# Five stage transitions worked in two groups of 256 tokens, with two weight remainders per transition on GpSimd

## What is computed

```python
# first block (FF = 2816; a 3x3 depthwise convolution over the 8 x 64 grid of tokens)
x  = x + g1 * (merge(...) @ w_out)                         # output stage
h2 = rmsnorm(x) * gain * (1 + scale) + shift               # transition A
x  = x + g2 * ((silu(z1) * z2) @ ffn_down)                 # z1, z2 = conv(h2 @ ffn_up)
x  = rmsnorm(x) * final_g                                  # sums of the "final norm"
# second block: retention with context keys, SwiGLU, short convolution, SwiGLU
ax = rms_norm(x, norm_mix) * (1 + sc) + sh                 # transition B
x  = x + g1 * ((silu(g) * o) @ w_o)                        # four heads
fx = modulate(rms_norm(x))                                 # transition C
x  = x + g2 * swiglu(fx, w1, w3, w2)
ax = modulate(rms_norm(x))                                 # transition D
x  = x + g1 * ((b_gate * conv3(c_gate * xv)) @ w_conv_out) # b, c, xv = ax @ w_conv_in
fx = modulate(rms_norm(x))                                 # transition E
x  = x + g2 * swiglu(fx, w1, w3, w2); out = rms_norm(x) * final_norm
```

## Time and profile before

| | us |
|---|---|
| median of 3 runs | 2410.75 |
| the profiled execution | 2411.24 |
| its span, first to last instruction | 2409.5 |

### The profile page before, as it was taken

The page is one execution under the profiler, slowest core; times in us unless marked ns, Lnnn a source line. Parts: engine busy times, 40 slices in busy tenths (PEclk is TensorE's granted clock), DMA queues, the critical chain, the costliest instruction groups (busy, mean ns, idle before and its releaser), DMA issues.

```text
span 2409.5 us, 29333 instructions
## 1 busy us (share of the span) xinstructions
PE 2305.6 (96%) x10276; PEld 1862.6 (77%) x10276; DVE 1395.6 (58%) x2056; ACT 874.8 (36%) x1168; POOL 162.6 (7%) x96
## 2 busy tenths in 40 slices
PE   7999999989999989999999998999998998999998
PEld 3788888768887868787778776888886886888886
DVE  4556856669999766654745547555435445333322
ACT  4533433245554333323323234443223233443322
POOL 0000000026664000000000000000000000000000
PEclk9999999999999999999999998999999999999999
DMA  6442214413334624142332323666532332333322
GB/s 270 131 136 74 71 57 151 152 57 105 89 102 140 192 80 146 55 129 88 104 116 74 106 79 124 192 190 199 157 93 65 105 96 63 105 94 104 96 88 70
DMA packets 72944, 273.82 MB, mean 114 GB/s; under 512 B 8096, under 2 KB 8480, under 8 KB 71456
## 3 DMA queue, kind: packets, MB, share of 16 engines
q1 hardware_dynamic: 53424, 199.74, 26.7%
q10 hardware_dynamic: 19440, 72.96, 9.6%
HBM read 270.57 MB, written 2.10 MB: 113 GB/s over the span
## 4 chain that ended last, share of the span: by engine, by line
PE 90%; DVE 5%; issue 2%; ACT 2%; DMA 1%; ACTq 0%; DVEq 0%; POOL 0%; SPq 0%
PE bank L424 85%; PE bank L765 1%; PE bank L862 1%; DVE rstd L472 1%; DVE rv_lo L1979 0%; DVE hx_lo L480 0%; PE bank L455 0%; DMA ident<-in_ident 0%; DVE tnorm L487 0%; PE bank L659 0%; PE bank L457 0%; DVE rstd L1799 0%; DVE std L449 0%; DVE rt L1930 0%; PE bank L944 0%
## 5 line engine op out<-in xcount | busy, mean ns | idle before, releaser
L424 PE MATMUL bank<-hx_hi,w_hi 128*128 128x512 f32 x1792 | 711.6, 397 | 40.2 <-DVE hx_lo L480 35.0
L424 PE MATMUL bank<-hx_hi,w_lo 128*128 128x512 f32 x1792 | 704.0, 393 | 0.0
L424 PE MATMUL bank<-hx_lo,w_hi 128*128 128x512 f32 x1792 | 703.9, 393 | 0.0
L383 DVE TENSOR_TENSOR w_lo<-w_raw,w_hi 128x1024 fp32r<-128x1024 f32 x306 | 374.8, 1225 | 495.2 <-ACT w_hi L375 488.9
L375 ACT ACTIVATE w_hi<-w_raw 128x1024 fp32r<-128x1024 f32 x350 | 369.0, 1055 | 458.1 <-PE bank L424 416.3
L424 PEld LDWEIGHTS bank<-hx_hi,w_hi 128*128 128x128 f32 x1792 | 340.7, 190 | 116.6 <-issue 41.1
L424 PEld LDWEIGHTS bank<-hx_hi,w_lo 128*128 128x128 f32 x1792 | 339.9, 190 | 72.4
L424 PEld LDWEIGHTS bank<-hx_lo,w_hi 128*128 128x128 f32 x1792 | 340.6, 190 | 71.0 <-issue 1.2
L1859 DVE SCALAR_TENSOR_TENSOR bank<-zpad,cols,bank 128x512 f32<-128x512 f32 x352 | 233.8, 751 | 11.7 <-ACT bank L1388 11.7
L424 PE MATMUL bank<-hid_hi,w_hi 128*128 128x512 f32 x528 | 210.1, 398 | 1.5 <-POOL hid_lo L2156 1.5
L424 PE MATMUL bank<-hid_lo,w_hi 128*128 128x512 f32 x528 | 209.8, 397 | 0.0
(11 more groups left out here) (305 smaller groups left out, 2752.3 us busy)
## 6 DMA issues: line engine op xcount, KB each, us to landing
w_raw<-in_wstream SPq DMA_DIRECT2D x350, 512.0 KB, 3.6
ada_raw<-in_ada_nk ACTq DMA_DIRECT2D x128, 512.0 KB, 3.7
ada_w<-in_ada_kn SPq DMA_DIRECT2D x8, 1024.0 KB, 18.8
dec<-in_dec ACTq DMA_DIRECT2D x4, 960.0 KB, 4.6
x_tok<-in_x SPq DMA_DIRECT2D x1, 2048.0 KB, 7.8
out_x<-out_tok SPq DMA_DIRECT2D x4, 512.0 KB, 4.0
crow<-in_crow SPq DMA_DIRECT2D x3, 512.0 KB, 23.1
ctx_tok<-in_ctx SPq DMA_DIRECT2D x1, 1024.0 KB, 9.9
```

Of the source, the lines that this page charges most:

```text
L383: nc.vector.tensor_tensor(w_lo[nb.at % RING][:], w_raw[nb.at % RAW][:], w_hi[nb.at % RING][:].bitcast(F32), ALU.subtract).then_inc(lo_read ...
L424: ins = nc.tensor.matmul(out_ap, s, m, start=first and at == 0, stop=last and at == n - 1)
```

## The change

The last output tile (B, D) or the last two (A, C, E) of the stage before a transition are worked in two halves of 256 tokens: first the first halves of all of them, then the second halves, which go to another bank (`bw`). The first half's update, squares, sums, root, reciprocal, scaling, `hx_hi` and `hx_lo` are done by themselves, in instructions 256 wide, and the sums of the first half stand in PE's queue after four k of the second halves. The next stage begins with three weight tiles in turn instead of two: for the first 256 tokens k = 0 and 1 of two tiles, then of the third, then k = 2 to 7 of all three, then all k for the second 256 tokens; the sums of the second half stand behind k = 2, and in B those of the final norm too. ACT and DVE have the second half's work between that of the first (`transition_act`, `transition_dve`). The root's table is loaded before the last squares. `w_lo` of the third and fourth blocks of the next stage (in C of the fourth alone) is written by GpSimd (`split_block`). The third tile of A goes to `by[0]`, that of B to `bw[0]`, and B's context keys come after all four tiles. The first round of the loops on ACT and DVE is written out where blocks are split elsewhere, the short convolution's loop is unrolled, and the final norm's scratch lies at other addresses. The transition at the start of the kernel and the one at its end stay.

```diff
+            def __init__(self, sems, scratch, past=(), last=0):
 
                 (self.sq_ready, self.summed, self.mm, self.root, self.rec, self.scaled, self.hi, self.lo) = sems
-                self.once, self.tiles, self.split_tiles, self.sums = n, KT * n, KT * split, (KT - 2) * n
                 self.sq, self.std, self.rooted, self.rstd = scratch
-
+                self.last = last
+                self.once = sum(2 if m else 1 for m in past)
+                self.tiles, self.halved = KT * self.once, sum(past)
+                self.squares, self.sums = sum(KT + m for m in past), sum(KT - 2 + (m == 2) for m in past)
...
+        last_halved = (0, 2, 1, 2, 1, 2, 0)
+        n1x, n2, nmx, nffn0, nmix1, nffn1, nf2 = (
+            Norm(shared, (sq, std, std, rstd), last_halved[:n], last_halved[n]) for n in range(7))
...
+        def half_sums_pe(pe, nm, h):
+
+            cut = HALF[h]
+            pe.wait_ge(nm.summed, nm.sums + KT - 2 + (h if nm.last == 2 else 0))
+            nc.tensor.matmul(bn[:, cut], ones[:], nm.std[:, cut], start=True, stop=False)
+            pe.wait_ge(nm.sq_ready, nm.squares + KT + nm.last * h)
+            nc.tensor.matmul(bn[:, cut], ones[:], nm.sq[(KT - 1) % 2][:, cut], start=False, stop=True).then_inc(nm.mm, 1)
+
+        def last_tiles_pe(pe, nm, tiles, both=0, sums_at=3):
+
+            def step(at, n, h):
+                dst, second, terms = tiles[at]
+                b, t, hi, lo = terms[n]
+                if h == 0 and (n == 0 or t == 0):
+                    pe.wait_ge(lo_ready, b.count(1))
+                wh, wl = wtile(b, t)
+                return three((dst, second)[h][:, HALF[h]], [(wh, wl, hi[:, HALF[h]], lo[:, HALF[h]])],
+                             n == 0, n == len(terms) - 1)
+
+            for n in range(both):
+                for h in range(2):
+                    ins = step(0, n, h)
+                if tiles[0][2][n][1] == KT - 1:
+                    ins.then_inc(block_done, 1)
+            for at in range(len(tiles)):
+                for n in range(both, len(tiles[at][2])):
+                    ins = step(at, n, 0)
+                ins.then_inc(half_done, 1)
+            for at in range(len(tiles)):
+                for n in range(both, len(tiles[at][2])):
+                    ins = step(at, n, 1)
+                    if tiles[at][2][n][1] == KT - 1:
+                        ins.then_inc(block_done, 1)
+                    elif n == len(tiles[at][2]) - 1:
+                        ins.then_inc(wo_half, 1)
+                    if at == 0 and n == both + sums_at:
+                        half_sums_pe(pe, nm, 0)
+
+        def first_tiles_pe(pe, nm, jobs, beside=lambda k: None):
+
+            def step(job, k, h):
+                b, dst, ends = job
+                wh, wl = wtile(b, k)
+                ins = three(dst[:, HALF[h]], [(wh, wl, hx_hi[:, k, HALF[h]], hx_lo[:, k, HALF[h]])], k == 0, k == KT - 1)
+                if ends and h == 1 and k == KT - 1:
+                    ins.then_inc(block_done, 1)
+
+            for b, _, _ in jobs[:2]:
+                pe.wait_ge(lo_ready, b.count(1))
+            for k in range(2):
+                pe.wait_ge(nm.lo, nm.tiles + k + 1)
+                for job in jobs[:2]:
+                    step(job, k, 0)
+            pe.wait_ge(lo_ready, jobs[2][0].count(1))
+            for k in range(2):
+                step(jobs[2], k, 0)
+            for h in range(2):
+                for k in range(2 if h == 0 else 0, KT):
+                    pe.wait_ge(nm.lo, nm.tiles + KT * h + k + 1)
+                    for job in jobs:
+                        step(job, k, h)
+                    if h == 0 and k == 2:
+                        half_sums_pe(pe, nm, 1)
+                        beside(k)
+
+        def transition_act(act, nm, job, shift, first_block, eps=eps_col, scale=None, extra=None):
+
+            def last_square(j, h):
+                nc.scalar.activation(nm.sq[j % 2][:, HALF[h]], res[:, j, HALF[h]], ACT.Square,
+                                     scale=1.0 if scale is None else scale[:, j:j + 1]).then_inc(nm.sq_ready, 1)
+
+            def root(h):
+                act.wait_ge(nm.mm, nm.once + h + 1)
+                nc.scalar.activation(nm.std[:, HALF[h]], bn[:, HALF[h]], ACT.Sqrt, scale=1.0 / D, bias=eps[:])\
+                    .then_inc(nm.root, 1)
+
+            def hi(j, h):
+                act.wait_ge(nm.scaled, nm.tiles + KT * h + j + 1)
+                nc.scalar.activation(hx_hi[:, j, HALF[h]], tnorm[j % 2][:, HALF[h]], ACT.Identity, bias=shift(j))\
+                    .then_inc(nm.hi, 1)
+
+            last = range(KT - nm.last, KT)
+            nc.scalar.activation(table_col[:], eps_col[:], ACT.Sqrt)
+            act.wait_ge(nm.summed, nm.sums + KT - 3)
+            for n, j in enumerate(last):
+                act.wait_ge(half_added, nm.halved + n + 1)
+                last_square(j, 0)
+            root(0)
+            if nm is not nffn0:
+                split_hi(act, Block(first_block - 1))
+            hi(0, 0)
+            hi(1, 0)
+            if nm.last == 2:
+                act.wait_ge(y_free, job + KT - 1)
+                last_square(KT - 2, 1)
+            hi(2, 0)
+            hi(3, 0)
+            act.wait_ge(y_free, job + KT)
+            last_square(KT - 1, 1)
+            if extra is not None:
+                square(act, extra, KT - 1, res)
+            hi(4, 0)
+            hi(5, 0)
+            root(1)
+            split_hi(act, Block(first_block))
+            hi(6, 0)
+            hi(7, 0)
+            for j in range(KT):
+                hi(j, 1)
+
+        def half_update(dve, j, h, src, gate):
+
+            return nc.vector.scalar_tensor_tensor(out=res[:, j, HALF[h]], in0=src[:, HALF[h]], scalar=gate,
+                                                  in1=res[:, j, HALF[h]], op0=ALU.mult, op1=ALU.add)
+
+        def half_square(dve, nm, h):
+
+            dve.wait_ge(nm.sq_ready, nm.squares + KT - 1 + 2 * h)
+            dve.wait_ge(nm.summed, nm.sums + KT - 3 + h)
+            nc.vector.tensor_tensor(nm.std[:, HALF[h]], nm.std[:, HALF[h]], nm.sq[0][:, HALF[h]], ALU.add)\
+                .then_inc(nm.summed, 1)
+
+        def last_half_dve(dve, nm, gate):
+
+            for n, j in enumerate(range(KT - nm.last, KT)):
+                dve.wait_ge(half_done, nm.halved + n + 1)
+                half_update(dve, j, 0, by[j % 2], gate(j)).then_inc(half_added, 1)
+                if j == KT - 2:
+                    half_square(dve, nm, 0)
+
+        def transition_dve(dve, nm, done, gate, gain, shift, late=lambda j: None):
+
+            def rec(h):
+                dve.wait_ge(nm.root, nm.once + h + 1)
+                nc.vector.reciprocal(nm.rstd[:, HALF[h]], nm.std[:, HALF[h]]).then_inc(nm.rec, 1)
+                dve.wait_ge(nm.rec, nm.once + h + 1)
+
+            def scaled(j, h):
+                if j >= 2:
+                    dve.wait_ge(nm.lo, nm.tiles + KT * h + j - 1)
+                nc.vector.scalar_tensor_tensor(out=tnorm[j % 2][:, HALF[h]], in0=res[:, j, HALF[h]], scalar=gain(j),
+                                               in1=nm.rstd[:, HALF[h]], op0=ALU.mult, op1=ALU.mult).then_inc(nm.scaled, 1)
+
+            def lo(j, h):
+                dve.wait_ge(nm.scaled, nm.tiles + KT * h + j + 1)
+                dve.wait_ge(nm.hi, nm.tiles + KT * h + j + 1)
+                nc.vector.scalar_tensor_tensor(out=hx_lo[:, j, HALF[h]], in0=tnorm[j % 2][:, HALF[h]], scalar=shift(j),
+                                               in1=hx_hi[:, j, HALF[h]].bitcast(F32), op0=ALU.add, op1=ALU.subtract)\
+                    .then_inc(nm.lo, 1)
+
+            rec(0)
+            scaled(0, 0)
+            scaled(1, 0)
+            if nm.last == 2:
+                done(KT - 2)
+                half_update(dve, KT - 2, 1, bw[0], gate(KT - 2)).then_inc(y_free, 1)
+            lo(0, 0)
+            scaled(2, 0)
+            lo(1, 0)
+            scaled(3, 0)
+            done(KT - 1)
+            half_update(dve, KT - 1, 1, bw[1], gate(KT - 1)).then_inc(y_free, 1)
+            if nm.last == 2:
+                half_square(dve, nm, 1)
+            lo(2, 0)
+            for j in range(4, 7):
+                scaled(j, 0)
+                late(j)
+                lo(j - 1, 0)
+            rec(1)
+            scaled(7, 0)
+            lo(6, 0)
+            lo(7, 0)
+            for j in range(KT):
+                scaled(j, 1)
+                if j >= 1:
+                    lo(j - 1, 1)
+            lo(KT - 1, 1)
+            dve.wait_ge(nm.lo, nm.tiles + 2 * KT)
 
...
@@ hidden_down_pe
+                if nm is not None and ct == KT - 1:
+                    last_tiles_pe(pe, nm, [(dst, bw[1], [(b, t, hid_hi[:, k, :], hid_lo[:, k, :]) for b, t, k in tiles])],
+                                  HT - 2 * KT)
+                    continue
...
@@ swiglu_pe
-            pair_pe(pe, nm, [job(None, 0, kind) for kind in range(2)])
-            for kind in range(2):
```

(43 more changed lines are left out.)

217 lines of the change are left out of this document (117 added, 100 removed).

## The result

The changed kernel takes 2397.52 us (median of 5 runs, 2395.86 to 2398.24) against 2410.75 (five runs beside it, four from 2410.43 to 2411.6 and one of 2403.25): ratio 0.9948, 95% interval 0.9935 to 0.9961. The forecast was 2393 (2375 to 2404). The profiled execution is the one of 2395.86.

A forecast was written before the change was run, and what follows sets the result against it. PE is busy 96%, so only its standing or low clock can be won: transitions cost 67.6 us before, 33.5 after, gain 34.1, less 16.8 for GpSimd's hold, 17.3. 2411.24-17.3-0.5 = 2393 us, range 2375 to 2404.

The forecast's parts named there:

- the cover: At A, B, D, E PE's 6.62 us after the first halves just cover the chain to `hx_lo`; 10.35 us gap closes.
- Rival 3: Half matmuls in last and first tiles are bound by the weight load, spaced 0.19: 86 us, 2479; chance 0.05.
- GpSimd holds DVE: All transitions: DVE instructions reading two SBUF tensors stand until GpSimd's remainder ends; 16.8 us in all.
- Rival 1: At the transitions GpSimd's remainders don't hold DVE: gain 34.1, 2377 us; chance 0.2.
- The clock: PE's clock falls after idle times in A and C alone: 2.4 us in A, 2.6 in C.
- rival 2: Clock falls at each 1.9 us idle in A, B, D, E: 19.2 us, 2412; half of them 2403; chance 0.15.
- The last first half ends and DVE updates, H+0.7: A, B, D, E: DVE's first half update ends 0.7 us after H, PE having issued the last tiles' first halves.
- 0.2 for B's third tile: At B's first tiles, the context tile waits 0.2 us for DVE's `hc_lo`.
- rival 4: Half chains don't overlap as written, a wait the walk misses, 3 us in each transition: 2408; chance 0.08.
- the wait for ACT's bank: In A the fourth tile wants bank 1, freed after two ACT evacuations: PE stands 2.9 us instead of 0.65.
- They follow and give no further gain: In A's stage DVE's taps, 233.8 of PE's 243 us, follow with about 0.2 us to spare per tile.
- C's stalls: At C PE stalls 2.2+0.5 us ahead of the sums, 2.85 ahead of the first tile, 0.7 later: 6.3.

The follow-up runs named there:

- The first experiment: Changed kernel with each of GpSimd's nine remainders covering only 32 of its 1024 columns, all waits kept: 2380.5 us, 17.0 less than the changed kernel.

## Why the prediction was right

**The bound, the halves and the cover.** Half matmuls are spaced 0.12 in the last tiles and in the first ones, and D and E came close to the forecast (5.74 and 4.26 against 5.4 and 4.9). Rival 3 (weight load) is out.

**GpSimd holds DVE.** This was the step with the largest price (16.8) on the thinnest evidence, one row longer by 0.2 us. The first experiment measured 17.0. Place and kind (two SBUF inputs) were right, the size nearly so: the waits were 15.1 of the forecast 16.8, and the low clock in A made up the rest. Rival 1 is out: it said 2377 for the kernel as changed, and only without GpSimd's work is the time (2380.5) near that.

**The clock.** The forecast let it fall in A and C alone, and in this trace it did, for 3.2 and 2.1 us in A and 5.6 in C; B, D and E ran at 1.00. But that was partly luck, and rival 2 is neither right nor out (last section). By the spacing of the matmuls the falls cost 1.6 and 1.3 in A and 2.7 in C, where 0, 2.4 and 2.6 were taken.

**Where it failed: B.** 3.3 us were forecast, -0.3 came. The rows of DVE, then of PE:

```profile
875.95 1.75 DVE L660 RECIPROCAL c_rstd<-c_std 128x256 f32<-128x256 f32 x1 [5.55 <-ACT c_std L650]
...
880.38 0.48 DVE L580 SCALAR_TENSOR_TENSOR res<-bank,ada,res 128x256 f32<-128x256 f32 x1
...
887.53 0.47 DVE L614 SCALAR_TENSOR_TENSOR hx_lo<-tnorm,ada,hx_hi 128x256 fp32r<-128x256 f32 x1
...
889.36 0.48 DVE L580 SCALAR_TENSOR_TENSOR res<-bank,ada,res 128x256 f32<-128x256 f32 x1
...
879.92 0.70 PE L472 MATMUL bank<-std,ones 128*128 128x256 f32 x2 [0.89 <-DVE std L457]
...
889.94 0.35 PE L432 MATMUL bank<-hx_hi,w_hi 128*128 128x256 f32 x1 [3.41 <-DVE res L580]
```

"The last first half ends and DVE updates, H+0.7" doesn't hold in B: H is 878.76, and the update starts at 880.38, behind the context's reciprocal (875.95, it waits for ACT), a split and two adds. PE waits 0.89+0.90 for the sums. And "0.2 for B's third tile" missed that B's second tile takes the bank of the last down tile, which is given free together with the second half's update at 889.36, though `hx_lo` was there at 888.0: 1.8 us. The narrower bank wait took that away (3.41 to 1.62), and the moved reciprocal the 1.8 us for the sums. Both are rival 4 (a wait that the walk misses), in one transition of five.

**A, C and E.** A was forecast to gain 0.8 for a reason that doesn't hold: the wait for ACT's bank and the clock behind it were added as PE's loss, though the taps pace the stage. "They follow and give no further gain" should have been "their start sets the stage". The bank wait of 0.89 (A, E) and 1.08 (C) ahead of the last tile, from two `take_y` asked for together, was in no term. C's stalls came out at 1.08+0.51 ahead of the sums (2.7 forecast) and 2.72 (2.85).

**The sum.** Misses of -1.3 (A), -3.6 (B) and -0.6 (E) against +0.8 (C) and +0.4 (D) make 4.3 us too little gain. In the profiled run 2.4 us of luck in stretches with the same code covered more than half of it; the median, 1.7 above that run, has less of that luck. The rest of the 4.5 us between 2393 and 2397.5 is rounding and the 0.5 taken off for the median of before. So the range held although B's gain was missed whole, and not because every term was right.

## What to carry to other kernels

Before work is moved to GpSimd, look at what DVE runs beside it: put GpSimd's instruction beside DVE instructions with one SBUF input or beside a wait (here: one line on ACT, 6.6 us), else each one can cost nearly its length (here 1.9 us on the average for 2.4 us of work). When a stage transition is cut into halves, list for each first instruction of the next stage the bank it takes and what frees it, and ask for each bank as late as it is needed. A wait of the busiest engine is a cost only where no other engine paces the stage; see when that other engine starts and whether its span changes before removing the wait.
